# Causal key ranges, padded rotary heads, and softmaxes begun inside the projections ahead, in a two-block transformer kernel on one core

## What is computed

```python
# MLA and differential attention (272 keys, 256 queries)
mask = k_pos[None, :] <= q_pos[:, None]
...
s = jnp.einsum('bqhd,bkhd->bhqk', qb, k) * scale
p = _causal_softmax(s, q_pos, pos)
...
a = _causal_softmax(s1, q_pos, pos) - lam * _causal_softmax(s2, q_pos, pos)
...
# MoBA with one block: own keys only
s_own = jnp.where(rel >= 0, s_own, -jnp.inf)
...
# cross attention: no mask
p = jax.nn.softmax(s, axis=-1).astype(v.dtype)
```

## Time and profile before

| | before |
|---|---|
| median of 3 runs | 1471.72 us (1466.5 to 1472.68) |
| profiled execution, its own time | 1465.43 us |
| its span, first to last instruction | 1463.7 us |
| mean granted TensorE clock | 0.996 |
| TensorE matmul busy | 1422.5 us, 97% |
| VectorE, ScalarE, GpSimd busy | 999.1, 683.8, 544.4 us |
| first attention, first scores to spread of the sub-norm | 126.20 to 198.89 us |
| MoBA loop, to the first matmul of `B_OUT2` that needs its heads | 1171.54 to 1196.03 us |
| `B_XQ` to the first matmul of the FFN | 1220.09 to 1254.22 us |

### The profile page before, as it was taken

How to read it: one execution, slowest core, us unless ns; L and a number is a source line. 1 busy time by engine, 2 the same in 40 slices (tenths; PEclk the granted TensorE clock), 3 DMA queues, 4 the chain that set the end, 5 groups by cost and what they waited for, 6 DMA issues and landing times.

```text
span 1463.7 us, 31773 instructions
## 1 busy us (share of the span) xinstructions
PE 1422.5 (97%) x11218; PEld 1350.9 (92%) x11218; DVE 999.1 (68%) x2085; ACT 683.8 (47%) x1035; POOL 544.4 (37%) x255
## 2 busy tenths in 40 slices
PE   7999999999999999999999999999999998999997
PEld 6776688999999999999999999999989977899997
DVE  4524545889688888877676766666545754699987
ACT  4433654445454555543333333444455355555553
POOL 3313247778400000034444444444433434344541
PEclk9999999999999999999999999999999999999999
DMA  7421035667755555567777776556543513355552
GB/s 284 132 72 44 29 116 185 194 191 215 226 173 176 178 167 177 176 203 230 234 228 235 228 237 216 188 182 184 188 167 126 182 48 121 101 186 187 172 186 72
DMA packets 89995, 250.17 MB, mean 171 GB/s; under 512 B 10048, under 2 KB 35920, under 8 KB 89296
## 3 DMA queue, kind: packets, MB, share of 16 engines
q1 hardware_dynamic: 86112, 238.20, 51.4%
q10 hardware_dynamic: 3824, 11.17, 2.1%
HBM read 234.09 MB, written 15.24 MB: 170 GB/s over the span
## 4 chain that ended last, share of the span: by engine, by line
PE 92%; DVE 5%; ACT 2%; issue 1%; DMA 0%; ACTq 0%; POOL 0%; DVEq 0%
PE ps L1662 46%; PE ps L2058 28%; PE ps L2041 4%; PE ps L1934 2%; PE ps L1888 2%; PE ps L1677 1%; PE ps L1858 1%; PE ps L1908 1%; DVE big L1080 1%; DVE w_lo L1058 1%; PE ps L1710 1%; PE ps L1748 1%; PE ps L2014 0%; PE ps L1779 0%; DVE big L1072 0%
## 5 line engine op out<-in xcount | busy, mean ns | idle before, releaser
L499 POOL TENSOR_TENSOR w_lo<-raw,w_hi 128x1024 fp32r<-128x1024 f32 x193 | 490.2, 2542 | 796.6 <-ACT w_hi L603 796.5
L1662 PE MATMUL ps<-x_op,w_hi 128*128 128x256 f32 (+1 forms) x3968 | 738.8, 287 | 8.6 <-POOL x_op L511 2.8
L1662 PEld LDWEIGHTS ps<-x_op,w_hi 128*128 128x128 f32 x3968 | 617.7, 192 | 21.0 <-issue 10.1
L1662 PE MATMUL ps<-x_op,w_lo 128*128 128x256 f32 (+1 forms) x1984 | 562.5, 284 | 0.0
L603 ACT ACTIVATE w_hi<-raw 128x1024 fp32r<-128x1024 f32 x400 | 420.3, 1054 | 265.4 <-PE ps L2058 214.3
L2058 PE MATMUL ps<-h_op,w_hi 128*128 128x256 f32 x2400 | 426.8, 280 | 2.4 <-DVE h_op L1612 2.4
L1662 PEld LDWEIGHTS ps<-x_op,w_lo 128*128 128x128 f32 x1984 | 379.8, 191 | 0.0
L2058 PEld LDWEIGHTS ps<-h_op,w_hi 128*128 128x128 f32 x2400 | 368.4, 189 | 3.1 <-issue 1.8
L1058 DVE TENSOR_TENSOR w_lo<-raw,w_hi 128x1024 fp32r<-128x1024 f32 x207 | 263.6, 1273 | 121.1 <-ACT w_hi L603 121.0
L2058 PE MATMUL ps<-h_op,w_lo 128*128 128x256 f32 x1200 | 337.8, 282 | 0.0
L2058 PEld LDWEIGHTS ps<-h_op,w_lo 128*128 128x128 f32 x1200 | 225.4, 188 | 0.0
(11 more groups left out here) (273 smaller groups left out, 1058.8 us busy)
## 6 DMA issues: line engine op xcount, KB each, us to landing
raw<-blocks SPq DMA_DIRECT2D x404, 512.0 KB, 3.6
early_store<-kv_mem SPq DMA_DIRECT2D x96, 128.0 KB, 1.7
work<-early_store SPq DMA_DIRECT2D x96, 128.0 KB, 3.6
big<-consts ACTq DMA_DIRECT2D x2, 1336.0 KB, 6.3
big<-h_t ACTq DMA_DIRECT2D x4, 272.0 KB, 4.1
big<-bias_lines ACTq DMA_DIRECT2D x8, 136.0 KB, 2.5
bias_lines<-route_t ACTq DMA_DIRECT2D x4, 264.0 KB, 2.5
res<-mem_t SPq DMA_DIRECT2D x1, 1024.0 KB, 8.6
```

The costliest lines, as they stand in the source:

```text
L499: pool.tensor_tensor(w_lo[:, s, :], raw[:, s, :], w_hi[:, s, :].bitcast(F32), ALU.subtract).then_inc(sem("lo_pool"), 1)
L1662: mm = pe.matmul(ps[:, m_bank, 0:T], w, x, start=(k == 0 and j == 0), stop=(k == last and j == 2))
```

## The change

1. **Causal ranges.** `seen(u, t)` is the number of keys that query tile t can see: 144 and 272 for MLA and the differential maps, 128 and 256 for MoBA, all for the cross attention. Scores, mask, maximum, exponential and normalisation work on that range; where one instruction treated both tiles there are now two. `key_tiles(u)` gives for each key tile the first query that sees it, rounded down to 32; transposes and `weigh` leave out the queries ahead. For MLA that makes widths of 256, 160 and 32 columns in place of three times 256, and the whole fits one bank (448 columns), so `probs_out` is one copy. Two of the five transposes then read 32 partitions only. For MoBA the widths are 256 and 128.
2. **Padded heads.** The rotary heads' queries and keys lie in tiles of 128 rows, of which rows 96 to 127 are zero (memsets on GpSimd at the start, 2048 and 2176 columns), and the score matmuls read 128 rows in place of 96. GpSimd also zeroes 3 x 112 columns of the scores before its first `normalise`.
3. **Entries.** MoBA's second scores, `soft_in`, `soft` and both inverses move between the last input blocks; the mix tiles' high and low parts move into the loop (after units 3 and 4). For the cross attention `scores(U_X)` and `scores(U_X + 1)` stand in the middle of the second `B_XQ` block.
4. **Low and high parts.** Before the cross attention GpSimd makes only the low part of block `B_XO`, after the operand is done; `B_FFN` and the next come after its loop. ScalarE's rounding of the last three of these blocks, and VectorE's low part of `B_XO + 1`, move into the cross-attention loop.
5. **Tables.** Square-root or exponential tables are loaded ahead of their use, at six places.
6. **Matmuls of ones.** `ENTRY_WARM` is 6 for `U_MLA` (new), none for MoBA, 4 for `U_X`; 5 and 4 are added between the first transposes, and 12 before the sub-norm's spread become 8.
7. **PEER.** `split` writes its product to PSUM (`weighted`, banks 2 and 3) in place of SBUF.

```diff
+        q_full = area(HEADS, NQ)
+        k_full = area(HEADS, NK)
+        q_mla, k_mla = q_full[0:QK], k_full[0:QK]
...
+        weighted = ps[:, 2:4, 0:NQ]
...
-        ENTRY_WARM = {U_MOBA: 13, U_X: 15}
+        CROSS_HI_AT = {U_X + 1: 2, U_X + 2: 3, U_X + 3: 4}
+        ENTRY_WARM = {U_MLA: 6, U_X: 4}
+        def seen(u, t):
+            keys = units[u]["keys"]
+            return keys if units[u]["kind"] == "xattn" else min(keys, keys - NQ + P * (t + 1))
+        def key_tiles(u):
+            at = 0
+            for j in range(-(-units[u]["keys"] // P)):
+                if units[u]["kind"] == "xattn":
+                    first = 0
+                else:
+                    first = max(0, P * j - (units[u]["keys"] - NQ)) // 32 * 32
+                yield j, min(P, units[u]["keys"] - P * j), first, at
+                at += NQ - first
...
# GpSimd
-                    pool.tensor_tensor(s, s, row_inv[:, u % 3, :].unsqueeze(2).to_broadcast([P, 2, n]), ALU.mult
-                                       ).then_inc(sem("probs_normed"), 1)
+                    for t in range(2):
+                        s = scores_sb[:, u % 3, t, 0:seen(u, t)]
+                        ins = pool.tensor_tensor(s, s, row_inv[:, u % 3, t:t + 1].to_broadcast([P, seen(u, t)]), ALU.mult)
+                    ins.then_inc(sem("probs_normed"), 1)
...
+            pool.memset(flat2(q_full), 0.0)
+            pool.memset(flat2(k_full), 0.0)
...
-            los(pool_at[0], B_FFN + 2)
+            los(pool_at[0], B_XO)
+            pool.wait_ge(sem("x_odd"), KT // 2 * operands(R_XATTN))
+            los(B_XO, B_FFN)
             normalise(U_X, U_END)
+            los(B_FFN, B_FFN + 2)
...
# ScalarE
-                if x["keys"] > NQ:
-                    act.activation(probs_t[0:N_META, o % 2, 2, :], ps[0:N_META, out_bank(o), NQ:2 * NQ], ACT.Copy)
-                act.activation(flat2(probs_t[:, o % 2, 0:2, :]), ps[:, 6, :], ACT.Copy).then_inc(sem("probs_ready"), 1)
+                n = probs_width(u)
+                act.activation(probs_t[:, o % 2, 0:n], ps[:, 6, 0:n], ACT.Copy).then_inc(sem("probs_ready"), 1)
...
+                    if s == U_MOBA - 1:
+                        act.activation(eps[:, 5:6], eps[:, 4:5], ACT.Sqrt)
...
+                    if s == U_MOBA + 3:
+                        mix_hi()
+                    if s in CROSS_HI_AT:
+                        his(B_XO + CROSS_HI_AT[s])
...
             root(R_XATTN, NQ)
+            act.activation(eps[:, 5:6], eps[:, 4:5], ACT.Exp)
+            soft(U_X)
+            attention(U_X, U_END, 1)
             his(B_FFN + 2)
-            attention(U_X, U_END)
-            his(B_FFN + 2)
+            sqrt_table()
...
# VectorE
+            evacuate_in2(22)
+            soft_in(U_MOBA + 1)
+            inverse(U_MOBA)
+            evacuate_in2(23)
+            inverse(U_MOBA + 1)
             evacuate_in2(24)
-            los(B_OUT2 + 2)
-            for w, (src, a) in enumerate(((conv_y, 0), (y_gla, 6))):
...
-            attention(U_MOBA, U_X, True)
+            attention(U_MOBA, U_X, 2, 2)
...
-                los(B_XQ + j + 3)
-            attention(U_X, U_END)
+                if j == 0:
+                    soft_in(U_X)
+            attention(U_X, U_END, 1)
...
# TensorE, turn(u) and weigh(u)
+                for j, k, first, at in key_tiles(u):
+                    for t in range(first // P, 2):
+                        r = max(first - P * t, 0)
+                        a = at + P * t + r - first
+                        mm = pe.transpose(ps[0:k, 6, a:a + P - r], scores_sb[r:P, u % 3, t, P * j:P * j + k], ident[r:P, r:P])
...
+                    mm = pe.matmul(ps[rows, out_bank(o), first:NQ], v, probs_t[0:k, o % 2, at:at + NQ - first],
+                                   start=(t == 0), stop=(P * t + k == x["keys"]), skip_group_check=True)
...
-            projections(B_XQ, M_XQ, 2, NQ, operand(R_XATTN))
+            projections(B_XQ, M_XQ, 1, NQ, operand(R_XATTN))
+            project(At(B_XQ + 1), (M_XQ + 1) % 2, NQ, bank_free(M_XQ + 1), None, range(KT // 2))
+            pe.wait_ge(sem("bank_free"), M_XQ + 1)
+            pe.wait_ge(sem("kv_back"), 16)
+            scores(U_X)
+            scores(U_X + 1)
+            project(At(B_XQ + 1), (M_XQ + 1) % 2, NQ, None, None, range(KT // 2, KT))
             pe.wait_ge(sem("bank_free"), M_XO)
```

147 lines of the change are left out of this document (80 added, 67 removed).

## The result

| | before | changed |
|---|---|---|
| median | 1469.11 us (1465.63 to 1472.68, 4 runs) | 1447.49 us (1446.42 to 1449.79, 4 runs) |
| ratio | | 0.9864, 95% interval 0.9839 to 0.989 |
| span of the profiled execution | 1463.7 us | 1444.9 us |
| mean granted clock | 0.996 | 0.999 |

A forecast was written before the change was run, and what follows sets the result against it. TensorE, holding 92% of the chain, was taken as the bound. Gains of 9.6 (first attention), 1.7 (MoBA) and 5.3 (cross attention), 16.6 us off 1465.43, gave 1448.8; half of 6.3 added made 1452, range 1444 to 1461.

The forecast's parts named there:

- (a): First attention, eight MLA units: shorter scores and weighing take a unit from 3.39 to 2.67 us, 5.8 us saved.
- The gap of 0.18 ahead of `weigh`: MLA unit, between scores and weighing: 0.18 us taken as a wait for the copies and expected to vanish.
- (b): First attention, four differential pairs: each saves 0.5 to 0.8 us, limited by VectorE; 3.0 us together.
- (c): First attention: loading the square-root table before the spread saves 0.8 of 1.28 us; new ones at the entry give nothing.
- (d): MoBA: the loop's period falls from 2.65 to 2.5 us, saving 1.2, and the entry saves 0.5; 1.7 us.
- the entry 3.17 less the work that now lies bare there: MoBA's entry: 3.17 us of ones go, mix work and an extra unit's share lie bare; 0.5 us saved.
- The rival in which MoBA gets free: MoBA: TensorE alone sets the period, 4.5 to 6 us more gained, total 1446; chance 0.10.
- (e): Cross attention: first transposes 6.5 us earlier, 1.3 given back for roundings and a low part; net 5.3 us.
- (f): Memsets at the start and PEER's product in PSUM: hidden by idle time and room, no time gained or lost.
- Dearer row changes: First attention's short transposes: moving to 32 partitions and back costs 0.3, not 0.09 us; total 1461, chance 0.08.
- PSUM for `weighted`: PEER: VectorE becomes slow on the PSUM operand and TensorE waits 128 times; total 1474.6 us, chance 0.04.
- The clock: MoBA's entry and cross attention: fewer ones let the clock fall, 3.1 us each, 1458 with two falls; chance 0.12.

The follow-up runs named there:

- Rounding to 64: The changed kernel with a key tile's first query rounded down to 64 in place of 32: 1450.70 us.
- PSUM variant: The kernel before with one edit alone, PEER's product of activation and gate in PSUM: 1467.15 us median, ratio 1.0009.
- Both undoings: The changed kernel with cross scores behind both query blocks again, 1451.47 us; and with low and high parts ahead of the cross attention again, 1451.69 us.

## Why the prediction was right, and where it was not

**What bounds it.** Right. Each stage that moved is one of the three named, and the others agree to 0.1 us. The total of 18.7 against 16.6 forecast hides errors of both signs: 1.7 too much for the first attention, 1.8 and 1.9 too little for MoBA and the cross attention. That they cancel in part is luck.

**(a) MLA, 5.8 forecast.** From the first transposes to the last of the eight units the gain is 30.68 - 27.21 = 3.47 for seven units, 0.50 each: 4.0 for eight. The step that failed is "The gap of 0.18 ahead of `weigh` is a wait for the copies ...; I let it go". Scores with that gap came to 0.90, not 0.70; `weigh` (1.07 against 1.08) and `turn` (0.93 against 0.89) were right. Two units tell what the gap was, one behind the transposes and one behind sixteen other matmul instructions, by whose end the copies are long done. TensorE and the copy before:

```profile
141.60 1.08 PE L1888 MATMUL ps<-big 96*128 96x272 f32 x4
142.61 1.65 PE L1934 MATMUL ps<-big,work 128*64 128x256 f32 x6
...
145.38 0.57 ACT L804 ACTIVATE big<-ps 128x512 f32<-128x512 f32 x1
```

and TensorE after the change:

```profile
140.75 0.87 PE L1956 MATMUL ps<-big 128*128 128x144 f32 x4
141.55 1.14 PE L1998 MATMUL ps<-big,work 128*64 128x256 f32 x6
```

Before, scores and `weigh` start 1.01 apart here and 1.10 behind transposes, where the copy ended at 145.95 and `weigh` started at 146.00. So half of the gap, 0.09, was the wait for the copies, and it did go. The other half is no wait: it is in the 1.01 (four instructions are 0.92), in the 0.80 after the change (0.70 by columns) and in the 1.01 of such a unit with scores over all keys, and it stands where the scores give way to 64 columns of values. And 0.10 came anew, the 0.90 against 0.80 after the change, where the last transposes of 32 rows give way to the scores. Rounding to 64 shows the same place with 0.15 for one change of rows that is there or isn't. So a unit pays twice more the price that I had put on the transposes alone. The rule that I cited against the short transposes, in the Trainium skill, "TensorEngine Tiling (Array Packing)", Key Properties, that a change of tiling mode drains TensorE, fits both places. I applied it to the new transposes only, and not to a gap that stood in the rows already. That each of the two is such a drain is argued from these readings and was not isolated.

**(b) Differential maps, 3.0.** The pair is 178.35 - 172.95 = 5.40 us, from 6.15: 0.75, within 0.5 to 0.8. From the last MLA unit's transposes to the last transposes of all, 26.35 became 23.83, 2.5.

**(c) Table and entry, 0.8.** From the last transposes to the spread 7.82 became 6.53, 1.3, in which some 0.5 of the last `weigh` lies: 0.8 for the table. The entry, which I gave nothing, gained 0.65 (7.84 to 7.19 us from first scores to first transposes). The ones aren't the reason, as without them it is 7.07; they cost 0.1 there at most. Whether they give something is open: the one execution without them lost 2.9 us by a clock fall in this stage, and the profiled executions of the kernel before and of its PSUM variant, which have no ones there either, had no fall there.

**(d) MoBA, 1.7.** 3.5 measured. The step that failed is "the entry 3.17 less the work that now lies bare there". From last scores to first transposes 3.39 went, and only 1.0 came back ahead of it, as the second scores between the blocks: 2.4, against 0.5. I had counted VectorE's 1.29 for the mix tiles as bare at the entry, where they weren't any more. Their cost came in the loop, which I put at 1.2 of gain: it gave 0.8 from first to last transposes. With the parts out of the loop another 1.3 to 1.6 comes. So the loop's own shorter rounds were worth more than I had worked out: from first to last transposes 17.96 us became 15.86 with the parts ahead and 15.61 with the low parts on GpSimd, and all but 0.8 of this was lost to the work put into it. The rival in which MoBA gets free is half true: two of the seven distances are 2.12 and one is 1.98, and from 1164.37 to 1166.49 TensorE has no stop at all (0.48 to the scores, 0.85 to `weigh`, 0.79 to the next transposes). So TensorE's own work is 2.12 and not the 1.9 that I had worked out, and with the low parts on GpSimd the mean distance of 2.23 is near it.

**(e) Cross attention, 5.3.** 7.2 measured. From the start of the norm's sums (L1694 before, L1762 after) to the first transposes 19.52 us became 11.55: 8.0 earlier, where 6.5 was forecast, and 0.8 is given back (1.3 forecast). The chain to the first exponential was right, 8.24 us against 8.2. The step that failed is that GpSimd's low part "holds its normalisation until about 1230". GpSimd after the change:

```profile
1211.30 2.39 POOL L521 TENSOR_TENSOR w_lo<-raw,w_hi 128x1024 fp32r<-128x1024 f32 x1 [4.05 <-DVE x_op L1140]
1217.61 1.18 POOL L559 TENSOR_TENSOR big<-big 128x256 f32<-128x256 f32 x2 [3.92 <-DVE big L1299]
```

The low part is done 3.92 us before the normalisation starts and holds nothing. The normalisation starts 10.3 us after the sums, where I had 11.2, and the transposes 1.2 after that, where I had 1.8: these are the 1.5 us.

What the 8.0 us are made of I hadn't asked, as I took them from one start of transposes to the other. GpSimd and TensorE before:

```profile
1231.98 1.04 POOL L536 TENSOR_TENSOR big<-big 128x512 f32<-128x512 f32 x1 [1.35 <-DVE big L1245]
1233.76 4.72 PE L1710 MATMUL ps<-ones 128*128 128x128 f32 x30
```

The first unit was normalised at 1233.02, 14.2 us after the sums (11.5 after the change): 2.7 us are the chain's. But its transposes began only at 1238.32, behind the third unit's scores and all 30 instructions of ones; after the change they begin 0.06 us behind the normalisation, with eight. These 5.2 us are TensorE's own. The clock has a part in them: it was at half from 1229.3 to 1236.1, of which TensorE worked from 1231.76 on, so 2.2 us were lost and not the 3.1 of the prediction, which counts the stop in. Most of the rest are 22 instructions of ones fewer, 2.7 us at the 0.122 each of the earlier trace rows. A run with fewer ones alone wasn't made. Both undoings show what a stop brings with it: 2.0 and 3.7 us of it, then 3.4 us at half clock.

**(f) At nothing.** Memsets and padding: right, starts agree to 0.1 us. PEER: the time of the changed kernel is as forecast, but the reason, that a split which "has room" may read either memory, is wrong. With SBUF the same kernel takes 9.2 us more. The room was that of the kernel before, in which none of the twelve held subtractions fell where TensorE needed its result. It was no property of the stage, and an edit elsewhere took it away. What shifted the engines against each other is not settled: the two kernels enter PEER 8 us apart, and other things around its first chunks moved as well.

**The rivals.** Dearer row changes: no, 0.09 to 0.15 each. PSUM for `weighted`: no wait, the other way round. The clock: not in the changed kernel's profiled execution, but it is real, as two of its four timed runs have a mean clock of 0.995 (0.999 in the profiled one) and lie 1.6 and 3.1 us above it. In MoBA, which has no ones any more, the clock fell in 4 of 12 profiled executions of the changed kernel and its variants (both with the product in SBUF, the one without ones, the one with late cross scores; none of them edited MoBA's loop), at a price of 2.4 to 3.9 us. The four are half of the eight executions whose MoBA loop is that of the changed kernel; the three with the mix tiles elsewhere and the one with scores over all keys had no fall, which is too few to tell. What decides it stays open, and ones inside that loop were not tried.

**The added half of 6.3 us** for the upper runs of before was a guess about the wrong thing: those runs are ones in which the clock fell, and the changed kernel's four runs had none of 6 us. Without it the sum, 1448.8, would have been within 1.3 of the median, by the luck named above.

## What to carry to other kernels

A gap that stands in the rows is to be explained before it is let go: here half of the 0.18 us ahead of `weigh` was the same price of changed rows and columns that was charged elsewhere. Matmuls that only fill a wait are to be laid against that wait: 30 of them began 0.7 us after the operand was ready, and held the transposes for 4.6 us. Slack that hides an edit belongs to how the engines stand to each other now, not to the stage; an operand moved to PSUM gave 0 in one kernel and 8 to 9 us in its successor. And work moved "into the idle time" of a loop has to be laid against the busiest engine's period: VectorE, at 2.0 of 2.1 us per unit, had none, while GpSimd waited for 5 us beside it.
